# Opening of a two-layer diffusion backbone: five modulation slots, later token loads, moved splits, and two stage entries reordered

## What is computed

```python
for i in range(DEPTH):
    sh_l, sc_l, g_l = split(silu(c) @ ada_w[i] + ada_b[i], 3)      # and sh_c, sc_c, g_c from c_ctx
    u_lat = rmsnorm(h_lat, norm_g[i]) * (1.0 + sc_l) + sh_l        # and u_ctx
    # layer 0: windowed attention with a sink || Hyena: long convolutions whose filters
    #          come from a small sine network, are scaled by a decay and divided by sum |k|
    # layer 1: attention || multi-head latent attention
    o = mixer(u @ w_in) * silu(gate)
    h_lat = h_lat + g_l * (o @ w_out[i])                           # layer 0: h_ctx too
```

## Time and profile before

| what | value |
|---|---|
| runs | 1597.71, 1600.05, 1600.40 us |
| profiled execution, its own time | 1598.85 us |
| its span | 1597.0 us |
| PE busy | 1499.4 us (94% of the span) |
| DVE, ACT, POOL busy | 1025.8, 572.6, 220.2 us |
| granted TensorE clock, mean | 0.974 of full |
| read from HBM, written | 256.36 MB, 14.68 MB |

### The profile page before, as it was taken

One profiled execution on the slowest core, in us unless ns is written; L12 is line 12 of the kernel. 1 busy time (PEld: TensorE's weight loads), 2 busy tenths in 40 slices (PEclk: granted clock), 3 DMA queues, 4 the chain that ended last, 5 costly groups with the idle time before them and its releaser, 6 DMA issues.

```text
span 1597.0 us, 19274 instructions
## 1 busy us (share of the span) xinstructions
PE 1499.4 (94%) x7747; PEld 1188.6 (74%) x7747; DVE 1025.8 (64%) x1200; ACT 572.6 (36%) x798; POOL 220.2 (14%) x244
## 2 busy tenths in 40 slices
PE   3887999999999999999988999989999888999998
PEld 0323688888887878788776788867798776788998
DVE  3552599889888877777665554555567555565543
ACT  2342322222222433433223311144257555455432
POOL 1000133333332000000000234430000000000000
PEclk8997999999999999999998999989999999999999
DMA  9677655454544544343457666532243322233563
GB/s 356 233 280 301 247 185 200 158 186 161 194 156 169 178 171 152 139 175 142 139 191 257 220 217 224 182 126 79 79 132 106 99 73 73 73 106 106 201 209 145
DMA packets 68938, 272.29 MB, mean 170 GB/s; under 512 B 10929, under 2 KB 21361, under 8 KB 48369
## 3 DMA queue, kind: packets, MB, share of 16 engines
q1 hardware_dynamic: 48226, 193.46, 34.6%
q0 software_dynamic: 20624, 77.60, 13.8%
HBM read 256.36 MB, written 14.68 MB: 170 GB/s over the span
## 4 chain that ended last, share of the span: by engine, by line
PE 80%; DVE 6%; DMA 6%; ACT 4%; issue 3%; POOL 1%; SPq 0%; DVEq 0%; ACTq 0%; POOLq 0%
PE banks L1001 20%; PE banks L995 19%; PE banks L998 19%; DMA raw<-in_ev_tiles 2%; DMA hT<-in_hT 2%; PE banks L1166 2%; PE banks L1153 2%; PE banks L2075 2%; PE banks L2009 1%; ACT wh L955 1%; PE banks L977 1%; PE banks L1987 1%; PE banks L978 1%; PE banks L980 1%; PE banks L2054 1%
## 5 line engine op out<-in xcount | busy, mean ns | idle before, releaser
L995 PE MATMUL banks<-xh,wh 128*128 128x512 f32 (+1 forms) x1840 | 633.4, 360 | 12.1 <-ACT wh L955 8.3
L998 PE MATMUL banks<-xl,wh 128*128 128x512 f32 (+1 forms) x1840 | 618.0, 351 | 0.3 <-DVE xl L1776 0.2
L995 PEld LDWEIGHTS banks<-xh,wh 128*128 128x128 f32 x1840 | 350.4, 190 | 65.6 <-issue 17.6
L998 PEld LDWEIGHTS banks<-xl,wh 128*128 128x128 f32 x1840 | 350.4, 190 | 51.6 <-issue 4.1
L1001 PE MATMUL banks<-xh,wl 128*128 128x512 f32 (+1 forms) x1840 | 360.9, 349 | 0.3 <-DVE wl L965 0.3
L965 DVE TENSOR_TENSOR wl<-raw,wh 128x2048 fp32r<-128x2048 f32 (+1 forms) x124 | 280.9, 2266 | 93.8 <-ACT wh L955 93.8
L1001 PEld LDWEIGHTS banks<-xh,wl 128*128 128x128 f32 x1840 | 300.8, 189 | 44.9 <-DVE wl L965 0.7
L955 ACT ACTIVATE wh<-raw 128x2048 fp32r<-128x2048 f32 (+1 forms) x124 | 235.4, 1899 | 235.4 <-PE banks L1001 176.8
L369 DVE SCALAR_TENSOR_TENSOR ada_acc<-ada_w,cond,ada_acc 128x1024 f32<-128x1024 f32 x120 | 159.3, 1328 | 7.3 <-DMA ada_w<-in_ada_rest 5.1
L392 POOL DMA_DIRECT2D ada_w<-in_ada_rest x128 | 70.2, 549 | 596.5 <-DVE ada_acc L381 390.8
L381 DVE SCALAR_TENSOR_TENSOR ada_acc<-ada_w,cond,ada_acc 128x1024 f32<-128x1024 f32 x90 | 125.2, 1392 | 0.0
(11 more groups left out here) (281 smaller groups left out, 1578.7 us busy)
## 6 DMA issues: line engine op xcount, KB each, us to landing
ada_w<-in_ada_rest POOLq DMA_DIRECT2D x128, 512.0 KB, 3.8
raw<-in_ev_tiles SPq DMA_DIRECT2D x52, 1024.0 KB, 6.9
raw<-in_od_tiles SPq DMA_DIRECT2D x34, 1024.0 KB, 4.8
ada_ring<-in_ada_first SPq DMA_DIRECT2D x32, 1024.0 KB, 7.3
raw<-in_out_tiles SPq DMA_DIRECT2D x32, 1024.0 KB, 4.9
hT<-in_hT POOLq DMA_DIRECT2D x4, 1024.0 KB, 24.6
spectra<-kstage POOLq DMA_DIRECT2D x8, 512.0 KB, 8.5
kf<-spectra SPq DMA_DIRECT2D x4, 1024.0 KB, 4.8
```

What stands on the lines that cost most here:

```text
L995: nc.tensor.matmul(out, wh[:, k, :], b.xh[:, seg, k, :], start=(k == 0), stop=False)
L998: nc.tensor.matmul(out, wh[:, k, :], b.xl[:, seg, k, :], start=False, stop=False)
```

## The change

- The modulation ring has five slots. The fourth lies over a part of `core` that is loaded later, the fifth over the last four blocks of `xh`, which are written last. SP waits for the piece five before.
- POOL loads token block q only when piece 1 + q is used.
- The bias of the Hyena filters comes in four rows of 512 (2 KB), one for each filter, on POOL's queue: row 0 behind `decay`, the others when the filter before has used its own. Filter 0 waits for row 0 too.
- Tile 1's weights are loaded at piece 16, with no wait for the tap.
- Squares move to ticks 7 and 8, behind the row copy in ACT's tick; scaling to ticks 11, 12, 13 and 15 (four blocks each); the first shift and split from tick 9 to 14.
- The high split of tile 0 is at tick 18 (when filter 2's spectra are stored), of tile 1 at 22; the low splits are at 21 and 22. Pairs are at ticks 23 to 28.
- A `product` with `ready` waits for the low weights first and does all three products of a block together.
- Second norm: ACT squares the last tile in place of POOL, PE adds it in a second set of sums, and DVE's weight split stands ahead of the reciprocal.

```diff
--- before.py
+++ after.py
@@ -244,9 +244,11 @@
     b.flt_abs = put("flt_abs", "HL", 24 * K, [P, 4, 512])
-    b.hybias = put("hybias", "RAW", 8 * K, [1, 2, BW])
+    b.hybias = put("hybias", "C", 10 * K, [1, 512])
     b.lag = put("lag", "EX", 4 * K, [P, 2, 512])
-    b.ada_ring = put("ada_ring", "ADA", 0, [P, 3, 4, 512])
+    ring = [put(f"ada_ring{i}", "ADA", 8 * i * K, [P, 2048]) for i in range(3)] + [put("ada_ring3", "C", 2 * K, [P, 2048])]
+    b.ada_ring = [r[:].rearrange("p (h k n) -> p h k n", h=2, k=2) for r in ring]
+    b.ada_ring.append(put("ada_ring4", "U", 12 * K, [P, 2, 4096])[:, :, 0:1024].rearrange("p h (k n) -> p h k n", k=2))
     b.condw = put("condw", "S", 32 * K, [P, KT, 32])
@@ -434,10 +437,12 @@
 STAGE_TICK = (0, 2, 3, 4)
-SQUARE_TICK = 3
-SPLIT_TICK = 23
-PAIR_TICK = {25: (0, 1), 26: (2, 3), 27: (4, 5), 28: (6, 7), 29: (8, 9), 30: (10,), 31: (11,)}
-SCALE_TICK = {7: range(0, 6), 8: range(6, 12), 9: range(12, 16)}
+SQUARE_TICK = 7
+SPLIT_HIGH = {18: 0, 22: 1}
+SPLIT_LOW = {21: 0, 22: 1}
+SHIFT_TICK = {14: 0, 17: 1, 25: 2}
+PAIR_TICK = {23: (0, 1), 24: (2, 3), 25: (4, 5), 26: (6, 7), 27: (8, 9), 28: (10, 11)}
+SCALE_TICK = {11: range(0, 4), 12: range(4, 8), 13: range(8, 12), 15: range(12, 16)}
@@ -467,24 +472,22 @@
     def _(sp):
-        sp.dma_start(b.core[:, 0:4 * P], g.core[:, 0:4 * P]).then_inc(s.ident_in, 16)
+        sp.dma_start(b.core[:, 0:4 * P], g.core[:, 0:4 * P]).then_inc(s.rows_in, 16)
         sp.dma_start(b.rows[:], g.rows).then_inc(s.rows_in, 16)
...
         for p in range(ADA_PIECES):
-            if p >= 3:
-                sp.wait_ge(s.ada_pe_used, p - 2)
-            sp.dma_start(b.ada_ring[:, p % 3].rearrange("p k n -> p (k n)"), g.ada_first[p]).then_inc(
-                s.ada_pe_landed[p % 3], 16)
+            if p >= ADA_RING:
+                sp.wait_ge(s.ada_pe_used, p - ADA_RING + 1)
+            sp.dma_start(b.ada_ring[p % ADA_RING], g.ada_first[p].rearrange("p (h k n) -> p h k n", h=2, k=2)).then_inc(
+                s.ada_pe_landed[p % ADA_RING], 16)
             if p == 2:
                 sp.dma_start(b.lag[:], g.lag.rearrange("p (a c) -> p a c", a=2)).then_inc(s.core_in, 16)
-                sp.dma_start(b.hybias[:], g.hy_bias).then_inc(s.core_in, 16)
                 sp.dma_start(b.sink[:], g.ev_sink.to_broadcast((P, HEADS))).then_inc(s.core_in, 16)
...
                 load_raw(sp, b, s, 0, l0_weights(g, 0), (KT, P))
-            if p == 20:
-                sp.wait_ge(s.flt_sd, 12)
+            if p == 16:
                 load_raw(sp, b, s, 1, l0_weights(g, 1), (KT, P))
-        sp.wait_ge(s.core_in, 48)
+        sp.wait_ge(s.core_in, 32)
         for i in (2, 3):
@@ -495,10 +498,20 @@
         pool.dma_start(b.decay[:], g.decay.rearrange("p (a c) -> p a c", a=2)).then_inc(s.flt_in, 16)
+
+        def bias_row(f):
+            if f > 0:
+                pool.wait_ge(s.flt_sd, 3 * f)
+            pool.dma_start(b.hybias[:], g.hy_bias[:, f // 2, 512 * (f % 2):512 * (f % 2) + 512]).then_inc(s.flt_in, 16)
+
+        bias_row(0)
         for q in range(4):
+            pool.wait_ge(s.ada_pe_used, 2 + q)
             pool.dma_start(b.hT[:, 4 * q:4 * q + 4, :], g.hT[:, 4 * q:4 * q + 4, :]).then_inc(s.x_in, 16)
...
             o, c = f // 2, f % 2
+            if f < 3:
+                bias_row(f + 1)
             pool.wait_ge(s.k_scaled, 4 * (f + 1))
@@ -508,8 +521,7 @@
-        pe.wait_ge(s.ident_in, 16)
-        pe.wait_ge(s.rows_in, 32)
+        pe.wait_ge(s.rows_in, 48)
         nc.tensor.transpose(ps[6][:, 0:128], b.rows[:, 0, :], b.ident)
@@ -519,11 +531,11 @@
             grp, r = divmod(p, 4)
-            pe.wait_ge(s.ada_pe_landed[p % 3], 16 * (p // 3 + 1))
+            pe.wait_ge(s.ada_pe_landed[p % ADA_RING], 16 * (p // ADA_RING + 1))
             if r == 0 and grp > 0:
...
             for q in range(4):
-                last = nc.tensor.matmul(ps[7][32 * q:32 * q + 32, :], b.condw[:, 4 * r + q, :], b.ada_ring[:, p % 3, q, :],
+                last = nc.tensor.matmul(ps[7][32 * q:32 * q + 32, :], b.condw[:, 4 * r + q, :], b.ada_ring[p % ADA_RING][:, q // 2, q % 2, :],
                                         start=(r == 0), stop=(r == 3), skip_group_check=True)
@@ -657,12 +669,6 @@
                 keep_spectra(filter_stage(tick - 1)[0], (0, 2))
-            if tick in (SQUARE_TICK, SQUARE_TICK + 1):
-                act.wait_ge(s.x_in, 64)
-                for k in range(8 * (tick - SQUARE_TICK), 8 * (tick - SQUARE_TICK) + 8):
-                    if k >= 8:
-                        act.wait_ge(s.x_summed, k - 7)
-                    a.activation(b.xsq[k % 8 // 4][:, k % 4, :], b.hT[:, k, :], ACT.Square).then_inc(s.x_squared, 1)
             if tick > 0 and filter_stage(tick - 1) is not None and filter_stage(tick - 1)[1] == 0:
@@ -684,18 +690,23 @@
                     s.norm_root, 1)
-            if tick % 8 == 1 and tick > 8:
-                shift(tick // 8 - 1)
+            if tick in SHIFT_TICK:
+                shift(SHIFT_TICK[tick])
             if tick % 4 == 3:
...
                 a.activation(b.arow[:, grp % 2], ps[7], ACT.Copy).then_inc(s.row_kept, 1)
-            if tick == SPLIT_TICK:
-                act.wait_ge(s.k_out, 128)
-                split_high(nc, act, b, s, 0)
-                split_high(nc, act, b, s, 1)
+            if tick in (SQUARE_TICK, SQUARE_TICK + 1):
+                act.wait_ge(s.x_in, 64)
+                for k in range(8 * (tick - SQUARE_TICK), 8 * (tick - SQUARE_TICK) + 8):
+                    if k >= 8:
+                        act.wait_ge(s.x_summed, k - 7)
+                    a.activation(b.xsq[k % 8 // 4][:, k % 4, :], b.hT[:, k, :], ACT.Square).then_inc(s.x_squared, 1)
+            if tick in SPLIT_HIGH:
+                act.wait_ge(s.k_out, 96 + 32 * SPLIT_HIGH[tick])
+                split_high(nc, act, b, s, SPLIT_HIGH[tick])
         shift(3)
@@ -769,11 +780,11 @@
                 dve.wait_ge(s.flt_sum, 2 * (f + 1))
-                dve.wait_ge(s.core_in, 48)
+                dve.wait_ge(s.flt_in, 80 + 16 * (f + 1))
                 turned = ps[4].rearrange("p (i q w) -> p i q w", i=4, q=4)[:, :, :, 0]
...
                 chain(v.reciprocal(b.inv_sum[:, o, 4 * c:4 * c + 4], b.inv_sum[:, o, 4 * c:4 * c + 4]))
-                chain(v.tensor_tensor(b.tap[:], ps[5][0:1, :], b.hybias[:, o, 512 * c:512 * c + 512], ALU.mult))
+                chain(v.tensor_tensor(b.tap[:], ps[5][0:1, :], b.hybias[:], ALU.mult))
                 dve.wait_ge(s.flt_sd, 3 * f + 2)
@@ -816,13 +827,15 @@
                 v.tensor_tensor(b.hT[:, k, :], b.hT[:, k, :], ps[0], ALU.mult).then_inc(s.norm_scaled, 1)
-            if tick % 8 == 1 and tick > 8:
-                split(tick // 8 - 1)
-            if tick == SPLIT_TICK:
-                split_low(nc, dve, b, s, 0)
-                split_low(nc, dve, b, s, 1)
+            if tick in SHIFT_TICK:
+                split(SHIFT_TICK[tick])
+            if tick in SPLIT_LOW:
+                if SPLIT_LOW[tick] == 0:
+                    dve.wait_ge(s.k_mm, 16)
+                    dve.wait_ge(s.flt_sum, 8)
+                split_low(nc, dve, b, s, SPLIT_LOW[tick])
         modulation(ADA_GROUPS - 1)
-        dve.wait_ge(s.core_in, 48)
+        dve.wait_ge(s.core_in, 32)
         chain(v.tensor_scalar(b.nsink[:], b.sink[:], -1.0, None, ALU.mult))
@@ -862,9 +875,14 @@
     def _(pe):
-        pe.wait_ge(s.squares_summed, KT)
+        pe.wait_ge(s.squares_summed, KT - 1)
         for j in range(4):
-            last = nc.tensor.matmul(ps[6][:, j:j + 1], b.nsum[:, j * P:(j + 1) * P], b.ones[:, 0:1], start=True, stop=True)
+            nc.tensor.matmul(ps[6][:, j:j + 1], b.nsum[:, j * P:(j + 1) * P], b.ones[:, 0:1], start=(j == 0), stop=False,
+                             skip_group_check=True)
+        pe.wait_ge(s.x_squared, KT + 1)
+        for j in range(4):
+            last = nc.tensor.matmul(ps[6][:, j:j + 1], b.hres[:, 0, j * P:(j + 1) * P], b.ones[:, 0:1], start=False,
+                                    stop=True, skip_group_check=True)
         last.then_inc(s.norm_summed, 1)
@@ -885,6 +903,8 @@
         split_high(nc, act, b, s, t + 1)
+        act.wait_ge(s.out_added, 2 * KT)
+        nc.scalar.activation(b.hres[:, 0, :], b.hT[:, KT - 1, :], ACT.Square).then_inc(s.x_squared, 1)
         act.wait_ge(s.norm_summed, 2)
@@ -906,9 +926,9 @@
                                    s.norm_rstd, 1)
+        split_low(nc, dve, b, s, t + 1)
         dve.wait_ge(s.norm_root, 2)
         v.reciprocal(b.nri[:, 0:4], b.nrs[:, 0:4]).then_inc(s.norm_rstd, 1)
-        split_low(nc, dve, b, s, t + 1)
         dve.wait_ge(s.norm_spread, 2)
@@ -989,12 +1009,18 @@
     wl = b.wl[:, t % 2, :].rearrange("p (k m) -> p k m", m=P)
+    if ready is not None:
+        pe.wait_ge(s.lo_done, t + 1)
+        for k in range(KT):
+            pe.wait_ge(ready[0], k + 1)
+            nc.tensor.matmul(out, wh[:, k, :], b.xh[:, seg, k, :], start=(k == 0), stop=False)
```

(14 more changed lines are left out.)

15 lines of the change are left out of this document (6 added, 9 removed).

## The result

The changed kernel takes 1585.58 us (median of 4 runs, 1583.4 to 1589.07) against 1600.22 beside it (4 runs): ratio 0.9906, 95% interval 0.9889 to 0.9924, or 15 us less (12 to 18). I forecast 6.1 less, so the sign was right and the size was not. The profiled execution took 1583.4 us, span 1581.6; its granted clock averages 0.980, before it was 0.974.

What follows compares the result with a forecast made beforehand. After 180 us TensorE is nearly always busy; the opening, a chain of handovers between three engines, had time to give. Opening 2.5, first output tile 2.4 and second norm 1.2 make 6.1 us off 1598.85: 1592.8, range 1585 to 1600.

Steps and rivals of the forecast that it cites:

- The entries: Changes outside the first 180 us: first output tile of layer 0 (2.4 us less) and second norm (1.2 less).
- Piece 3 no longer waits for the last two blocks ... so I take 29.2: Modulation piece 3, with token blocks queued behind pieces, lands at 29.2 us in place of 34.8.
- X: Start of tick 4: 34.3 us forecast (bounds 32.4 to 34.9), 41.4 before.
- S1: Start of filter 1's matmuls: 47.9 us forecast, 58.7 before.
- S2: Start of filter 2's matmuls: 74.8 us forecast, 82.6 before.
- S3: Start of filter 3's matmuls: 98.1 us forecast, 100.5 before.
- I take 1.0 off: Landing of the last filter spectra's stores in DRAM, before the pairs: 1.0 us sooner, bounds 0 and 3.8.
- the opening: First 180 us of the kernel: forecast 2.5 us less, bounds 0.9 and 7.2.
- Given back behind the pairs: Pieces, transposes and a row copy left for behind the pairs' start: 3.3 us lost again.
- the opening gives more: Rival: piece 3 at 27.3, quicker stores, norm and tile at upper ends: 1585.9 us; chance 0.28.
- Tokens too late: Rival: token blocks compete with pieces and land at 67 us, squares wait: 1605.9 us, slower; chance 0.07.
- the handovers between ticks 11 and 16 eat the gain: Rival: ticks 11 to 16 cost 2.5 us more than walked: 1595.2 to 1596.9 us; chance 0.20.

Runs made afterwards that it cites:

- second sample: Trace of the changed kernel run once more without an edit, beside the experiments: 1586.60 us, ratio 0.9919 to the kernel before.
- Tokens first: Changed kernel with all four token blocks issued at the start as before, five slots kept: 1594.51 us, ratio 0.9951 to the kernel before.
- ring of three: Changed kernel with three slots in the modulation ring in place of five: 1590.81 us, ratio 0.9924 to the kernel before.
- entries alone: Kernel before with only the first output tile's and second norm's changes, opening as before: 1596.14 us, ratio 0.9969 to the kernel before.

## Why the prediction was wrong, point by point

- **The entries and their kind were right.** Entries forecast 3.6, measured 5.0 (3.0 to 7.0). Tile 0: 2.4 forecast; the length from layer 0's attention through tile 0 fell by 2.3 and 1.9. Norm: 1.2 forecast, scaling 2.05 and 0.84 earlier behind the last product in the two samples. No table load stands there, as layer 1's rows had said. The 2.66 us taken as its price were too high in any case: the kernel's own load (1.28 us at 1044.12, before) has the next ACT instruction 0.01 us behind it, so it would have cost 1.3.
- **The step that failed: "Piece 3 no longer waits for the last two blocks ... so I take 29.2".** I let the blocks follow "one per piece" from 20.5 on and counted two ahead of piece 3. But the release of the second block is the use of piece 2, and that piece's matmuls end only when the 10.24 us wait before 34.80 begins, at 24.56; the row was in front of me. So one block at most is in flight, and it was not ahead: issued at 19.8, it landed at 28.2, behind piece 3. The term should have been four blocks and not two: 4.2 MB at 0.419 MB/us are 10.0 us where I had 5.0 to 5.6, and 34.8 - 10.0 = 24.8; measured 24.86, and some 25.5 in the second sample. X came 4.8 and 4.1 us before my 34.3, past its bound of 32.4. "Tokens first" shows the cause; "ring of three" shows that the slots are not. One term went the other way: piece 4 was to be "there by then", 2.5 us behind piece 3, but it landed some 4.6 behind it, beside the token block, and PE waited 2.24 us for it.
- **Clock.** I had left no term for an idle wait that no longer lowers the clock. Piece 3's matmuls, priced at half clock, ran at full (16 in 1.92 us). From X to S1 I took 13.6; measured were 13.76 at a mean granted clock of 0.88 and 12.18 at 1.00, and PE had no break in either.
- **S1 to S2** was walked at 26.9; 23.67 and 26.20 were measured (24.67 to 26.8 in the five other traces with tokens behind the pieces and the later squares). The step has two parts: first the way to piece 8, which waits for the row copy or for its own landing (5.53 and 6.42 us), and then work of PE without a break, whose length goes with the clock. My 20.9 us for it stand on 16.1 us of the kernel before, whose first 5.55 us ran at a mean clock of 0.69. The second part in the two samples, at a clock of 1.00 and of 0.91:

```profile
48.80:66.94 18.14, 18.14 (x106) 7.33 (x106) 3.35 (x8) 12.39 (x24) 0.52 (x1) 1.00 1.02 421
```

```profile
48.82:68.60 19.78, 19.78 (x106) 7.10 (x106) 2.46 (x8) 11.72 (x22) 0.52 (x1) 0.91 1.01 418
```

- **S2 to S3** at 23.3 was right: 22.55 and 22.77, with PE's wait of 2.6 at 2.82.
- **"I take 1.0 off" at the stores had the wrong sign.** From S3 to the landing I had 34.2; 37.23 and 35.80 were measured. The last store took 12.19 and 12.23 us instead of 10.5. The change is not the reason: it took 12.17 with three slots and 12.53 in "entries alone", which has the opening of before, so 11.47 was at the short end. The other 1.3 us of the first sample lie ahead of the store, where one group of eight filter matmuls took 5.15 us against 3.68 in the second sample, at a lower clock. Behind the landing, 4.3 forecast, 4.51 measured.
- **Given back behind the pairs:** 3.3 forecast, 2.6 and 1.9 measured.
- **Sum of the opening:** X 4.8, S1 to S2 3.2, S2 to S3 0.7, giving back 0.7 more than forecast; S3 to the landing 3.0, the splits 0.2 and X to S1 0.2 less: 6.0 beyond my 2.5, and 8.6 was measured. In the second sample the same terms make 6.4 beyond.
- **The signs.** One of the prediction's own signs of being wrong came: "a third filter before 95"; it began at 89.49 and 91.37. The two others did not (a first square waiting past 55, a table load in the norm).
- **The rivals.** The result lies where "the opening gives more" did (1585.9), but by another way, so that agreement is luck: its piece at 27.3 was still too late and its quicker stores did not come. "Tokens too late" did not happen, as the squares began at 48.55 without a wait, 2.5 us after the last block; with squares at tick 3 the same mechanism takes the whole gain. That the handovers between ticks 11 and 16 eat the gain was wrong.
- **Still open:** whether the last part, from the norm's pairs to the end, takes longer with the entries (509.3 to 511.8 us in the eleven traces with them, 508.2 and 509.0 in the two without); and how much of the 3.4 us between opening and output is real, of which the second sample kept 1.5.

## What to carry to other kernels

When a change ties a transfer to "piece n used", read from the trace when piece n is used, not when it is due, and count whole transfers that leave the path: here all four blocks did, and 10 us with them. Moving a transfer back pays only with the work that asks for it; either alone gave nothing. And where an engine waits long for the last input of a group, ask whether the group must wait as a whole: splitting the pairs by tile filled a wait of 15.7 us and was worth 14.9 us, as much as the entire change.
